# The first block of output weights split in four parts instead of one, in the last heads of a latent-attention layer

## The chip, the cores and the metric

The kernel runs as one program on one core of a Trainium2 chip. The metric is the device time of one execution in microseconds (us), as the median of several runs. Five engines work side by side, each through its own list of instructions in order, and they wait for one another on semaphores (counters that one engine raises and another waits for): TensorE (PE in the profile), VectorE (DVE), ScalarE (ACT), GpSimd (POOL) and SyncE (SP, which here issues DMAs).

## What is computed

The reference is a trunk of two layers over 512 tokens of width 1024, all in float32. The first layer is a multi-head latent attention with 16 heads, the second a sparse attention. The change lies at the end of the first layer's attention, where the output projection begins:

```python
def mla_mixer(h, pos, w_in, g_cq, w_uq, g_ckv, w_ukv, g_q, g_k, w_out):
    proj = h @ w_in
    c_q, c_kv, k_pe, z = jnp.split(proj, [...], axis=-1)
    q = (rms_norm(c_q, g_cq) @ w_uq).reshape(B, S, MLA_HEADS, MLA_QK)
    kv = (rms_norm(c_kv, g_ckv) @ w_ukv).reshape(B, S, MLA_HEADS, MLA_NOPE + MLA_V)
    ...
    o = causal_block_attention(q, k, v, MLA_QK ** -0.5)
    o = o.reshape(B, S, MLA_HEADS * MLA_V) * jax.nn.silu(z)
    return o @ w_out
```

`w_out` has 2048 rows (128 for each of the 16 heads) and 1024 columns.

## The kernel before

**Products in two pieces.** A float32 product is made of three matmuls (`mm3`, lines 97 to 99): each operand is split into a high piece (a rounded copy) and a low piece (the operand less its high piece), and high times high, high times low and low times high are summed. For weights the high piece `w_hi` is a copy on ACT and the low piece `w_lo` a subtraction on POOL. Weights come from memory in blocks of 512 rows by 512 columns, which lie in SBUF as 128 partitions by 4 times 512 elements (`KP` = 4); there are two buffers of each kind, `w_raw`, `w_hi`, `w_lo`, used in turn.

**Slots.** The attention runs in slots, one for each head and block of 128 queries: slot s is head s // 4 and query block s % 4, with 64 slots in all (`SLOTS0` = 64, `NT` = 4). Each engine has a function `step(s)` that writes out its share of slot s, and the list of its instructions is that of step after step; nothing else sets the order. The share of a late slot is:

- SP: two DMA transposes for the slot three further on, of queries (L1074) and keys (L1076), into `qkT`; the scores of that slot wait for them.
- PE: `scores(s)` (five matmuls into a bank, L97 to L99, L1255, L1256), in each fourth slot `values` of the head before (L1286), then `turn_probs(s - 1)` (transposes of the probabilities, L1269, and of the gate, L1276), which waits for the exponential of slot s - 1.
- DVE: `maximum(s)` (L2328: scores and mask, with the row minimum), `key_low` (L2309, L2311: the low pieces of a key tile, after ACT's high piece), `query_low`, `probs_out` or `gate` in every fourth slot, `turn_sum(s - 1)` (L2341).
- ACT: `key_high` (L1664), `probs_out(s - 1)` (L1685), `z_out` (L1696), `exponential(s)` (L1678).
- POOL: `scale_z` in the first two slots of a head (L2026), and factors for keys and queries in earlier slots.

**The first output products.** In the last eight slots the projections of queries and keys are over, and the output projection begins in the free banks. Its first block of weights, `mid[0]`, landed long before. ACT makes its high piece in slot 56 (`mid_high(0)`, L1741) and POOL its low piece in slot 57 (`mid_low(0)`, L2018), each as one instruction on 128 x 2048 elements. From slot 58 on ACT and DVE split one finished head's output in each slot into `o_hi` (L1751) and `o_lo` (L2354), and PE takes the first products of the first two token tiles in slot 60, behind the scores of slot 60 and ahead of `turn_probs(59)` (`first_products`, called by the table `first_at`). They wait for the whole low piece of the weights and for the first `o_lo`:

```python
if k == 0 and t == 0:
    pe.wait_ge(m_lo, 1)
    pe.wait_ge(q_scaled, H // 2 * NT)
...
if t == 0:
    pe.wait_ge(o_lo_made, k + 1)
```

In DVE's slot, `o_low` stands behind everything else of that slot, and so ahead of `maximum` of the next one; in ACT's slot, `o_high` stands behind the exponential.

Of the kernel before, what the change touches and what calls it, by code (L numbers as in the profile page):

```python
# [15 lines left out]
F32 = mybir.dt.float32  # L16
# [4 lines left out]
ACT = mybir.ActivationFunctionType  # L21
ALU = mybir.AluOpType
# [4 lines left out]
NT = SEQ // P  # L27
# [7 lines left out]
H = 16  # L35
# [30 lines left out]
KP = 4  # L66
# [35 lines left out]
def trunk(nc, x, positions, inv_freq, norm_g, mla_w_in, mla_g_cq, mla_w_uq, mla_g_ckv, mla_w_ukv,  # L102
          mla_g_q, mla_g_k, mla_w_out, nsa_w_in, nsa_g_q, nsa_g_k, nsa_pe_k, nsa_w1_k, nsa_w2_k,
          nsa_pe_v, nsa_w1_v, nsa_w2_v, nsa_w_out, out):
    with ExitStack() as whole:
# [30 lines left out]
        w_raw = [keep(f"w_raw{s}", [P, KP, CW]) for s in range(2)]  # L136
        w_hi = [keep(f"w_hi{s}", [P, KP, CW], F32R) for s in range(2)]
        w_lo = [keep(f"w_lo{s}", [P, KP, CW], F32R) for s in range(2)]
# [35 lines left out]
        with ExitStack() as layer:  # L174
            z_sb = at_slab("z_sb", 0, [P, NT, ZZ])
            with ExitStack() as ctx:
# [82 lines left out]
                q_done, q_squares, q_factors, q_scaled, q_rotated = (sem(n) for n in (  # L259
                    "q_done", "q_squares", "q_factors", "q_scaled", "q_rotated"))  # L260
                kv_done, k_squares, kv_out, k_factors, k_rotated = (sem(n) for n in (
                    "kv_done", "k_squares", "kv_out", "k_factors", "k_rotated"))
# [6 lines left out]
                SLOTS0, KV0, AHEAD = H * NT, -8, 3  # L269
# [1243 lines left out]
                def _(act):  # L1513
# [185 lines left out]
                    def step(s):  # L1699
                        if k_split(s) is not None:  # L1700
                            key_high(k_split(s))
                        if q_split(s) is not None:
                            query_high(q_split(s))
                        if q_tile(s - 1):
                            q_stats(q_tile(s - 1))
                        if k_tile(s):
                            kv_stats(k_tile(s))
                        if (q_weights(s) or 0) > 1:
                            split_q(q_weights(s))
                        if (k_weights(s) or 0) > 1:  # L1710
                            split_kv(k_weights(s))
                        if 1 <= s <= SLOTS0 and s % NT != 3:
                            probs_out(s - 1)
                        if s % NT in (1, 2) and NT < s < SLOTS0:
                            z_out(s - 1)
                        if 0 <= s < SLOTS0:
                            exponential(s)
                        if s == KV0 + 1:
                            z_leave(NB - 2)
                        if s == KV0 + 4:  # L1720
                            z_leave(NB - 1)
                        if s == KV0 + 5:
                            nc.scalar.activation(exp_junk[:, 0:1], minus_half[:, 0:1], ACT.Exp)
                        if s == SLOTS0 - 8:
                            mid_high(0)
                        if SLOTS0 - 6 <= s < SLOTS0 - 2:
                            o_high(s - SLOTS0 + 6)
                        if s == SLOTS0:
                            mid_high(1)
                        if s == SLOTS0 + 1:  # L1730
                            z_out(SLOTS0)

                    def mid_high(g):
                        act.wait_ge(m_landed[g % 2], 16 * (g // 2 + 1))
                        if g < 2:
                            act.wait_ge(kv_done, NT * (H - 1 + g))
                            act.wait_ge(q_done, NT * (H // 2 - 1 + g))
                        else:
                            act.wait_ge(m_done, NT * (g - 1))
                        width = mid[g][3]  # L1740
                        nc.scalar.activation(w_hi[g % 2][:, :, 0:width], w_raw[g % 2][:, :, 0:width],  # L1741
                                             ACT.Copy).then_inc(m_hi, 1)
# [169 lines left out]
                def _(pool):  # L1912
# [87 lines left out]
                    def rotate(m):  # L2000
# [11 lines left out]
                        nc.gpsimd.tensor_tensor(q[:, :, HALF0:ROPE], rot[:, 1], rot[:, 2], ALU.add).then_inc(q_rotated, 1)  # L2012
                        pool.wait_ge(q_rotated, m + 1)

                    def mid_low(g):
                        pool.wait_ge(m_hi, g + 1)
                        width = mid[g][3]
                        nc.gpsimd.tensor_tensor(w_lo[g % 2][:, :, 0:width], w_raw[g % 2][:, :, 0:width],  # L2018
                                                w_hi[g % 2][:, :, 0:width].bitcast(F32), ALU.subtract).then_inc(m_lo, 1)
# [8 lines left out]
                    def step(s):  # L2028
                        if s >= NT and s % NT < 2:
                            scale_z(s // NT - 1, s % NT)  # L2030
                        if s == KV0 + 4:
                            pool.wait_ge(z_used, NB)
                            o.link(nc.gpsimd.memset(no_low(2), 0.0))
                        if k_tile(s) is not None and s % 2:
                            k_factors_of(k_tile(s - 1))
                        if (q_tile(s - 1) or 0) >= NT - 1:
                            rotate(q_tile(s - 1))
                        if q_tile(s) is not None:
                            q_factor(q_tile(s))
                        if s == SLOTS0 - 7:  # L2040
                            mid_low(0)

                    slots(step)

# [555 lines left out]
```

## Time and profile before

| | |
|---|---|
| median of 3 runs | 854.2 us (853.71 to 854.38) |
| the profiled execution | 855.4 us |
| its span, first to last instruction | 853.6 us |
| mean granted TensorE clock | 0.994 of full speed |
| PE busy | 827.9 us, 97% of the span |
| DVE, ACT, POOL busy | 65%, 58%, 57% |

The profiled execution took 1.2 us more than the median of the runs, and 1.8 us of its time lie outside the span. A row of a timeline gives the start of an instruction in us from the span's start, its duration, engine, line, operation, output and inputs, and in brackets how long the engine had been idle before it and what ended that. A row with x4 merges four instructions that follow one another. An engine starts its next instruction a little before the one ahead has ended, so two rows of one engine may overlap by some 0.1 us.

### The profile page before, as it was taken

What the parts mean: (1) busy time and instruction counts of PE and PEld (TensorE: products, weight loads), DVE (VectorE), ACT (ScalarE), POOL (GpSimd) and SP (SyncE); (2) the same over time, 40 slices, a digit from 0 to 9 for tenths busy, and PEclk for the clock granted to TensorE, in tenths of its full rate; (3) what the DMA queues carried; (4) which work ended last, traced back from release to release, by engine and by line L of the source; (5) the groups of instructions that cost most, each with busy time, mean ns of one, the idle gap of its engine ahead of it and who ended that gap; (6) DMA issues with size and microseconds to landing.
All of it is one profiled execution on the core that took longest, in us unless ns stands there. A gap on an engine that the chain in (4) does not pass through costs nothing.

```text
span 853.6 us, 16381 instructions
## 1 busy us (share of the span) xinstructions
PE 827.9 (97%) x5785; PEld 686.6 (80%) x5785; DVE 552.8 (65%) x1544; ACT 493.1 (58%) x1183; POOL 484.2 (57%) x628
## 2 busy tenths in 40 slices
PE   6999998999999997999999999999999999999998
PEld 6999998888888885788888887778887677777786
DVE  4899988887887788461111113476789688888521
ACT  5446658887887886531334223444344889988620
POOL 2000315878887876344446343565674799999641
PEclk9999999899999999999999999999999999999999
DMA  6423232646456545242247222123312100100011
GB/s 220 134 88 96 80 115 82 132 118 117 94 126 118 124 83 130 69 141 78 74 119 156 94 65 82 51 99 105 98 51 99 50 2 3 51 2 3 2 50 49
DMA packets 100763, 73.60 MB, mean 86 GB/s; under 512 B 70197, under 2 KB 83786, under 8 KB 100682
## 3 DMA queue, kind: packets, MB, share of 16 engines
q1 hardware_dynamic: 100640, 72.55, 31.6%
q8 instruction: 46, 0.75, 0.4%
q14 instruction: 35, 0.29, 0.1%
q10 hardware_dynamic: 42, 0.01, 0.0%
HBM read 55.63 MB, written 2.10 MB: 68 GB/s over the span
## 4 chain that ended last, share of the span: by engine, by line
PE 79%; DVE 9%; ACT 5%; issue 3%; DMA 2%; SPq 1%; POOL 1%; ACTq 0%; DVEq 0%; POOLq 0%
PE bank L97 18%; PE bank L99 18%; PE bank L98 18%; PE bank L1286 3%; DVE w_lo L2198 2%; PE bank L510 2%; PE bank L492 2%; PE bank L519 2%; PE bank L511 2%; PE bank L1269 1%; DMA qkT<-k 1%; PE bank L599 1%; ACT prob L1678 1%; PE bank L600 1%; PE bank L598 1%
## 5 line engine op out<-in xcount | busy, mean ns | idle before, releaser
L2018 POOL TENSOR_TENSOR w_lo<-w_raw,w_hi 128x2048 fp32r<-128x2048 f32 (+1 forms) x26 | 118.4, 4554 | 124.2 <-ACT w_hi L1741 124.1
L97 PE MATMUL bank<-w_hi,h_hi 128*128 128x512 f32 (+3 forms) x472 | 171.4, 363 | 2.0 <-DVE h_lo L2118 1.0
L99 PE MATMUL bank<-w_hi,h_lo 128*128 128x512 f32 (+3 forms) x472 | 166.8, 353 | 0.0
L98 PE MATMUL bank<-w_lo,h_hi 128*128 128x512 f32 (+3 forms) x472 | 166.8, 353 | 0.0
L1741 ACT ACTIVATE w_hi<-w_raw 128x2048 fp32r<-128x2048 f32 (+1 forms) x26 | 49.2, 1892 | 94.0 <-PE bank L99 94.0
L97 PEld LDWEIGHTS bank<-w_hi,h_hi 128*128 128x128 f32 x472 | 88.8, 188 | 15.3 <-issue 3.7
L99 PEld LDWEIGHTS bank<-w_hi,h_lo 128*128 128x128 f32 x472 | 88.7, 188 | 11.5
L98 PEld LDWEIGHTS bank<-w_lo,h_hi 128*128 128x128 f32 x472 | 88.9, 188 | 10.1
L797 POOL TENSOR_TENSOR p<-kvr,p 128x512 f16<-128x512 f32 (+1 forms) x96 | 88.5, 942 | 10.3 <-ACT p L713 9.9
L97 PE MATMUL bank<-w_hi,c_hi 128*128 128x256 f32 (+1 forms) x224 | 78.6, 351 | 0.3 <-DVE w_lo L2277 0.2
L97 PE MATMUL bank<-w_hi,o_hi 128*128 128x512 f32 x192 | 77.7, 405 | 0.4 <-DVE o_lo L2354 0.4
L98 PE MATMUL bank<-w_lo,o_hi 128*128 128x512 f32 x192 | 76.2, 397 | 0.0
L99 PE MATMUL bank<-w_hi,o_lo 128*128 128x512 f32 x192 | 76.2, 397 | 0.0
L99 PE MATMUL bank<-w_hi,c_lo 128*128 128x256 f32 (+1 forms) x224 | 69.2, 309 | 0.0
L98 PE MATMUL bank<-w_lo,c_hi 128*128 128x256 f32 (+1 forms) x224 | 69.2, 309 | 0.0
L710 ACT ACTIVATE kvr<-bank,g_cols 128x512 f32<-128x512 f32 (+1 forms) x96 | 60.4, 630 | 7.6 <-PE bank L526 7.6
L847 DVE CUSTOM_DVE_ANT_0 scored<-bank,band 128x128 f32<-128x128 f32 (+3 forms) x128 | 56.1, 484 | 10.2 <-PE bank L492 10.2
L713 ACT ACTIVATE p<-bank,g_cols 128x512 f16<-128x512 f32 (+1 forms) x96 | 60.6, 631 | 0.0
L2328 DVE CUSTOM_DVE_ANT_0 below<-bank,band,g_cols 128x128 f32<-128x128 f32 (+1 forms) x64 | 34.8, 544 | 25.1 <-PE bank L1256 24.5
L97 PEld LDWEIGHTS bank<-w_hi,c_hi 128*128 128x128 f32 x224 | 43.1, 192 | 3.6 <-DVE w_lo L2277 0.5
L97 PEld LDWEIGHTS bank<-w_hi,o_hi 128*128 128x128 f32 x192 | 36.4, 189 | 8.8 <-issue 0.6
L98 PEld LDWEIGHTS bank<-w_lo,c_hi 128*128 128x128 f32 x224 | 43.1, 192 | 0.4
(362 smaller groups left out, 2336.7 us busy)
## 6 DMA issues: line engine op xcount, KB each, us to landing
w_raw<-in_nsa_w_in SPq DMA_DIRECT2D x10, 1024.0 KB, 5.0
w_raw<-in_mla_w_in SPq DMA_DIRECT2D x8, 1024.0 KB, 5.1
w_raw<-in_mla_w_out SPq DMA_DIRECT2D x8, 1024.0 KB, 5.1
w_raw<-in_nsa_w_in SPq DMA_DIRECT2D x8, 984.0 KB, 5.0
w_raw<-in_nsa_w_out SPq DMA_DIRECT2D x4, 1024.0 KB, 5.1
w_raw<-in_mla_w_uq SPq DMA_DIRECT2D x7, 576.0 KB, 4.5
w_raw<-in_mla_w_ukv SPq DMA_DIRECT2D x15, 256.0 KB, 2.9
w_raw<-in_mla_w_in SPq DMA_DIRECT2D x4, 704.0 KB, 5.7
```

What stands on the lines that cost most here:

```text
L97: nc.tensor.matmul(out, a[0], b[0], start=start, stop=False)
L98: nc.tensor.matmul(out, a[0], b[1], start=False, stop=False)
L99: return nc.tensor.matmul(out, a[1], b[0], start=False, stop=stop)
L492: nc.tensor.matmul(first_bank(k)[:, 0:nb * keys].rearrange("p (b c) -> p b c", b=nb), qT_hi[a][0:DK, tok], kT_hi[0:DK, b0:b0 + nb, n // HP ...
L710: nc.scalar.activation(p32(k, u), src, ACT.Exp, scale=score_scale[:, 0:1])
L713: nc.scalar.activation(piece_of(p1, n, u), src, ACT.Exp, scale=score_scale[:, 0:1]).then_inc(exp_done, 1)
L797: nc.gpsimd.tensor_tensor(piece_of(p2, n, u), p32(k, u), piece_of(p1, n, u), ALU.subtract).then_inc(sub_done, 1)
L847: last = nc.vector.tensor_tensor_reduce(scored[k % 2][:, w * keys:(w + 1) * keys], first_bank(k)[:, w * keys:(w + 1) * keys], band[:, SEQ ...
L1286: last = nc.tensor.matmul(o_bank[:, j * P:SEQ], kv_sb[:, h % 4 * NT + j, NOPE:WKV], probT[h % 2][:, j * ROW + j * P:j * ROW + SEQ], start= ...
L1741: nc.scalar.activation(w_hi[g % 2][:, :, 0:width], w_raw[g % 2][:, :, 0:width], ACT.Copy).then_inc(m_hi, 1)
L2018: nc.gpsimd.tensor_tensor(w_lo[g % 2][:, :, 0:width], w_raw[g % 2][:, :, 0:width], w_hi[g % 2][:, :, 0:width].bitcast(F32), ALU.subtract). ...
L2328: nc.vector.tensor_tensor_reduce(below[i % 2][:, 0:keys], score_bank[i % 2][:, 0:keys], band[:, SEQ - keys:SEQ], score_scale[:, 1:2], -LEA ...
```

## The change

The one high piece on ACT in slot 56 and the one low piece on POOL in slot 57 become four each, one k (128 x 512 elements) a slot, in slots 56 to 59 on both engines. ACT makes part k at the end of its slot 56 + k, ahead of `o_high` where that slot has one; POOL follows at the end of its own slot 56 + k. Only the first part on ACT waits for the block and for the buffers; only the fourth part on POOL raises `m_lo`, for which PE waits. Later blocks are as they were, but for POOL's count of `m_hi`.

```diff
@@ ScalarE, step(s)
-                        if s == SLOTS0 - 8:
-                            mid_high(0)
+                        if SLOTS0 - 8 <= s < SLOTS0 - 8 + KP:
+                            first_high(s - SLOTS0 + 8)
                         if SLOTS0 - 6 <= s < SLOTS0 - 2:
                             o_high(s - SLOTS0 + 6)
...
+                    def first_high(k):
+                        if k == 0:
+                            act.wait_ge(m_landed[0], 16)
+                            act.wait_ge(kv_done, NT * (H - 1))
+                            act.wait_ge(q_done, NT * (H // 2 - 1))
+                        width = mid[0][3]
+                        nc.scalar.activation(w_hi[0][:, k, 0:width], w_raw[0][:, k, 0:width], ACT.Copy).then_inc(m_hi, 1)
...
-                        if g < 2:
-                            act.wait_ge(kv_done, NT * (H - 1 + g))
-                            act.wait_ge(q_done, NT * (H // 2 - 1 + g))
+                        if g == 1:
+                            act.wait_ge(kv_done, NT * H)
+                            act.wait_ge(q_done, NT * H // 2)
...
@@ GpSimd
+                    def first_low(k):
+                        pool.wait_ge(m_hi, k + 1)
+                        width = mid[0][3]
+                        last = nc.gpsimd.tensor_tensor(w_lo[0][:, k, 0:width], w_raw[0][:, k, 0:width],
+                                                       w_hi[0][:, k, 0:width].bitcast(F32), ALU.subtract)
+                        if k == KP - 1:
+                            last.then_inc(m_lo, 1)
...
-                        pool.wait_ge(m_hi, g + 1)
+                        pool.wait_ge(m_hi, g + KP)
...
-                        if s == SLOTS0 - 7:
-                            mid_low(0)
+                        if SLOTS0 - 8 <= s < SLOTS0 - 8 + KP:
+                            first_low(s - SLOTS0 + 8)
```

The lists of PE, DVE and SP are the same as before. On ACT, slots 56 to 59 read as follows (`w_hi0`, `w_raw0`: the first buffers; `k16`: the key's high piece; `prob`: the exponential; `o_hi0`, `o_hi1`: the first two heads' outputs). Before:

```order
544 L1678 ACTIVATE prob_109,rowsum_64<-below0_107,negmax_63 128x128 [waits max_done]
545 L1741 ACTIVATE w_hi0<-w_raw0 128x2048 [waits q_done,kv_done,m_landed0]
546 L1664 ACTIVATE k16_1_72<-kv_sb_75,ms_k_67 128x128 [waits k_rotated,kv_out]
...
553 L1678 ACTIVATE prob_109,rowsum_64<-below0_107,negmax_63 128x384 [waits max_done]
554 L1751 ACTIVATE o_hi0_113<-z_sb_56 128x512 [waits o_free,q_done,kv_done]
555 L1678 ACTIVATE prob_109,rowsum_64<-below1_108,negmax_63 128x512 [waits max_done]
556 L1751 ACTIVATE o_hi1_114<-z_sb_56 128x512 [waits o_free]
557 L1685 ACTIVATE probT0_110<-bank2 128x4x128 [waits t_done]
```

and now:

```order
545 L1739 ACTIVATE w_hi0<-w_raw0 128x512 [waits q_done,kv_done,m_landed0]
...
549 L1678 ACTIVATE prob_109,rowsum_64<-below1_108,negmax_63 128x256 [waits max_done]
550 L1739 ACTIVATE w_hi0<-w_raw0 128x512
...
554 L1678 ACTIVATE prob_109,rowsum_64<-below0_107,negmax_63 128x384 [waits max_done]
555 L1739 ACTIVATE w_hi0<-w_raw0 128x512
556 L1759 ACTIVATE o_hi0_113<-z_sb_56 128x512 [waits o_free,q_done,kv_done]
557 L1678 ACTIVATE prob_109,rowsum_64<-below1_108,negmax_63 128x512 [waits max_done]
558 L1739 ACTIVATE w_hi0<-w_raw0 128x512
559 L1759 ACTIVATE o_hi1_114<-z_sb_56 128x512 [waits o_free]
```

The third part stands behind the exponential of slot 58, and the fourth behind that of slot 59; both stand ahead of an `o_hi`.

On POOL, the same slots (`z_sb`, `rinv`: `scale_z`). Before:

```order
368 L1995 TENSOR_TENSOR k16_1_72<-kpe_sb_59,ms_k_67 128x2x128 [waits x_landed1,x_landed0,k_factors]
369 L2026 TENSOR_TENSOR z_sb_56<-z_sb_56,rinv_65 128x2x128 [waits sum_turned] x2
370 L2018 TENSOR_TENSOR w_lo0<-w_raw0,w_hi0 128x2048 [waits m_hi]
371 L2026 TENSOR_TENSOR z_sb_56<-z_sb_56,rinv_65 128x2x128 [waits sum_turned] x4
372 L2018 TENSOR_TENSOR w_lo1<-w_raw1,w_hi1 128x2048 [waits m_hi]
```

and now:

```order
368 L2003 TENSOR_TENSOR k16_1_72<-kpe_sb_59,ms_k_67 128x2x128 [waits x_landed1,x_landed0,k_factors]
369 L2042 TENSOR_TENSOR z_sb_56<-z_sb_56,rinv_65 128x2x128 [waits sum_turned]
370 L2026 TENSOR_TENSOR w_lo0<-w_raw0,w_hi0 128x512 [waits m_hi]
371 L2042 TENSOR_TENSOR z_sb_56<-z_sb_56,rinv_65 128x2x128 [waits sum_turned]
372 L2026 TENSOR_TENSOR w_lo0<-w_raw0,w_hi0 128x512 [waits m_hi] x3
373 L2042 TENSOR_TENSOR z_sb_56<-z_sb_56,rinv_65 128x2x128 [waits sum_turned] x4
```

The second `scale_z` now stands behind the first part, and the last four behind the fourth part, which follows ACT's exponential of slot 59.

PE's list is unchanged; this is the place in it where the products stand, with the waits that they carry:

```order
2090 L1269 MATMUL bank2<-ident,prob_109 128x128 [waits zt_ready,pt_ready,exp_done]
2091 L1269 MATMUL bank2<-ident,prob_109 128x128 x2
2092 L97 MATMUL bank0<-qkT1_103 128x128 [waits max_done,x_landed0]
...
2097 L97 MATMUL bank4<-w_hi0,o_hi0_113 128x512 [waits o_lo_made,q_scaled,m_lo]
...
2103 L1269 MATMUL bank2<-ident,prob_109 128x128 [waits pt_ready,exp_done]
```

Nothing moved here: the transposes of slot 58's probabilities, the scores of slot 60, the six products, and behind them the transposes of slot 59's probabilities.

## Rows read from the trace of the kernel before

**Rows 1.** The profile's page: busy time by engine.

```profile
PE 827.9 (97%) x5785; PEld 686.6 (80%) x5785; DVE 552.8 (65%) x1544; ACT 493.1 (58%) x1183; POOL 484.2 (57%) x628
```

**Rows 2.** Waits, 325 to 370 us: waiter, releaser, total us, times, longest us.

```profile
PEld bank L1269 <- ACT prob L1678: 4.6, 3, 2.9
ACT prob L1678 <- DVE negmax L2328: 4.5, 3, 2.5
```

**Rows 3.** Timeline of POOL: the block's low piece; later, a piece of quarter size.

```profile
332.31 4.52 POOL L2018 TENSOR_TENSOR w_lo<-w_raw,w_hi 128x2048 fp32r<-128x2048 f32 x1 [0.50 <-ACT w_hi L1741]
...
684.08 1.26 POOL L788 TENSOR_TENSOR w_lo<-w_raw,w_hi 128x512 fp32r<-128x512 f32 x1
685.30 0.39 POOL L802 TENSOR_TENSOR c_s<-c_s,c_min 128x128 f32<-128x128 f32 x1
```

**Rows 4.** Timeline of DVE, slots 57 to 59.

```profile
332.56 4.42 DVE L2309 SCALAR_TENSOR_TENSOR k<-kv_sb,ms_k,k 128x128 f16<-128x128 f32 x1 [1.05 <-ACT k L1664]
336.90 0.27 DVE L2311 SCALAR_TENSOR_TENSOR k<-kpe_sb,ms_k,k 128x64 f16<-128x64 f32 x1
...
337.17 0.59 DVE L2328 CUSTOM_DVE_ANT_0 below<-bank,band,g_cols 128x384 f32<-128x384 f32 x1
...
337.69 0.34 DVE L2309 SCALAR_TENSOR_TENSOR k<-kv_sb,ms_k,k 128x128 f16<-128x128 f32 x1
...
339.07 0.69 DVE L2354 TENSOR_TENSOR o_lo<-z_sb,o_hi 128x512 fp32r<-128x512 f32 x1 [0.76 <-ACT o_hi L1751]
339.68 0.74 DVE L2328 CUSTOM_DVE_ANT_0 below<-bank,band,g_cols 128x512 f32<-128x512 f32 x1
```

**Rows 5.** Timeline of ACT, slots 56 to 59, and four copies in a row.

```profile
333.83 0.40 ACT L1664 ACTIVATE k<-kv_sb,ms_k 128x128 f16<-128x128 f32 x1
334.68 0.38 ACT L1685 ACTIVATE probT<-bank 128x256 f32<-128x256 f32 x1 [0.46 <-PE bank L1276]
334.96 0.38 ACT L1696 ACTIVATE zT<-bank 128x256 f32<-128x256 f32 x1
337.81 0.61 ACT L1678 ACTIVATE prob<-below,negmax 128x384 f32<-128x384 f32 x1 [2.47 <-DVE negmax L2328]
...
338.42 0.61 ACT L1751 ACTIVATE o_hi<-z_sb 128x512 fp32r<-128x512 f32 x1
340.46 0.72 ACT L1678 ACTIVATE prob<-below,negmax 128x512 f32<-128x512 f32 x1 [1.43 <-DVE negmax L2328]
...
341.19 0.61 ACT L1751 ACTIVATE o_hi<-z_sb 128x512 fp32r<-128x512 f32 x1
...
357.67 2.18 ACT L1751 ACTIVATE o_hi<-z_sb 128x512 fp32r<-128x512 f32 x4
```

**Rows 6.** Timeline of PE, slots 58 to 62.

```profile
333.35 0.33 PE L1256 MATMUL bank<-qkT 128*128 128x384 f16 x1
...
335.77 0.38 PE L1256 MATMUL bank<-qkT 128*128 128x512 f16 x1
338.57 0.55 PE L1269 MATMUL bank<-ident,prob 128*128 128x128 f32 x3 [2.42 <-ACT prob L1678]
...
339.90 0.77 PE L97 MATMUL bank<-w_hi,o_hi 128*128 128x512 f32 x1 [0.36 <-DVE o_lo L2354]
...
342.57 0.60 PE L1269 MATMUL bank<-ident,prob 128*128 128x128 f32 x4
...
347.12 0.53 PE L97 MATMUL bank<-w_hi,o_hi 128*128 128x512 f32 x1
...
348.64 0.38 PE L1269 MATMUL bank<-ident,prob 128*128 128x128 f32 x2
```

**Rows 7.** Stretches: busy us by engine, then granted TensorE clock, DMA share, GB/s.

```profile
339.40:340.20 0.80, 0.44 (x3) 0.33 (x2) 0.80 (x2) 0.00 (x0) 0.00 (x0) 0.50 0.73 149
...
344.20:345.00 0.80, 0.80 (x3) 0.37 (x2) 0.27 (x1) 0.50 (x1) 0.00 (x0) 1.00 0.19 37
```

**Rows 8.** Timeline of SP's queue: the key transpose for slot 60.

```profile
334.98 2.04 SPq L1076 DMA_TRANSPOSE qkT<-k  x1
```

## The prediction, made before the changed kernel ran

> **What bounds the kernel now.** I read the page first: PE is busy for 97% of the span [rows 1], so an edit matters only where PE stands idle or where it makes PE wait. Next come the waits around the slots that the change touches. Between 325 and 370 us PE's longest wait is for the exponential (ACT, L1678), and ACT's longest there is for DVE's maximum [rows 2]: 2.47 us on ACT and 2.42 us on PE end in one chain. The timelines then show what DVE did meanwhile. The low piece of a key, L2309, took 4.42 us [rows 4], where the next one of the same shape took 0.34. It started 0.25 us after POOL's low piece of the weight block (332.31, 4.52 us long [rows 3]), and DVE's next instruction started at 336.90, 0.07 us after POOL's end at 336.83. So a DVE instruction that reads two SBUF tensors stood still until POOL was done. Behind it stood the maximum of slot 58 (337.17), then the exponential (337.81), then PE's transposes (338.57) [rows 4, 5, 6]. The change makes four short holds out of the long one, and that should remove this wait. But the products of slot 60 (339.90) wait for the weights' low piece and for the first o_lo. Now the weights are ready at 336.83, three microseconds early, and o_lo ends last at 339.76 [rows 4, 6]. After the change the weights become ready only behind the exponential of slot 59. That is what the sum is about.
>
> **The path up to slot 58.** Part 0 on ACT starts where the large copy started; POOL's part 0 follows for 1.27 us, then scale_z. DVE's L2309 loses at most the rest of a part, and the maximum of slot 58 can start when its scores are ready, at 333.35 + 0.33 = 333.68 [rows 6]; with 0.59 us it ends near 334.3. Part 1 on ACT goes ahead of the key copy at 333.83, and 0.55 + 0.3 later, at about 334.7, the copy of turned probabilities starts as before, at 334.68, since it waits for PE [rows 5]. I cost this part at 0, with 0.1 at most. The second copy at 334.96 lasts 0.38, so the exponential of slot 58 starts at about 335.24 instead of 337.81: 2.57 us gained. Moving scale_z behind part 0 costs nothing, as PE's use of it is about 1.5 us away.
>
> **The path from there to the products.** In this order, each behind the one before:
> - The exponential with the read of its sum holds ACT for 338.42 - 337.81 = 0.61 us [rows 5], to 335.85.
> - Part 2 on ACT: four copies of 128 x 512 in a row took 2.18 us, 0.55 each [rows 5]; done at about 336.4. POOL starts 0.07 later, at 336.47.
> - Part 2 on POOL: 1.26 us for a subtraction of that shape [rows 3]; done at 337.73. The bounds are 4.52 / 4 = 1.13 and 1.3.
> - o_high(0) stands behind part 2 on ACT and ends near 336.98, when POOL is already in its part. o_low(0) reads two SBUF tensors (L2354), and as L2309 did it waits for POOL's end. L2309's 4.42 us, its own 0.34 counted from the end, reach to 336.98, 0.15 after POOL's end, so the work itself begins about 0.2 before POOL's recorded end. That puts o_low(0) at 337.6 to 338.3, and maximum(59) behind it at 338.25. Its scores had been ready since 336.15 [rows 6].
> - From the start of this maximum to that of its exponential: 340.46 - 339.68 = 0.78 us [rows 4, 5], giving 339.03. The exponential holds ACT for 341.19 - 340.46 = 0.73, to 339.76.
> - Part 3 on ACT 0.55 and hand-over 0.07: 340.4. Part 3 on POOL 1.26: 341.66. From a releaser's end to PE 339.90 - 339.76 = 0.14: the products start at 341.8.
>
> They started at 339.90. **The sum is +1.9 us for the start of the products.** The 2.57 us gained at slot 58 are spent, and 1.9 more, because the products had covered the maximum and the exponential of slot 59 before, and now wait for those, and then for one part on ACT and one on POOL.
>
> **What hangs on it.** Queued behind the products on PE are the transposes of slot 59's probabilities (342.57), which need only the exponential, and then scores and values. From 344.20 on PE is busy without a gap [rows 7], and so I find no place where the delay would be absorbed; the later blocks' pieces wait for PE. POOL's scale_z of the next head, behind part 3, ends by 342.6 and is needed some 5 us later. SP's list gates nothing new: the key transpose for slot 60 is issued at 334.98 for 2.04 us [rows 8], so scores(60) come at about 338.3, ahead of the products in any case. The extra 0.3 us of ACT work (4 x 0.55 against one copy) are in the terms above.
>
> **The clock.** The products of slot 60 ran at half the granted clock (0.50, the 1.2 GHz level), after the idle 2.42 us [rows 6, 7]. Six of them took 342.57 - 339.90 = 2.67 us, against 348.64 - 347.12 = 1.52 at full clock. In the new order PE is idle from about 336.5 to 338.3 and from 338.9 to 341.8, with one slot's scores between. So I expect the fall again, and its price of 1.15 us again, plus some 0.3 for the transposes and scores behind the products while the clock is still low. Bounds: -1.15 if the clock doesn't fall, +2.5 if values(14) too (about 2.3 us long at full clock) runs at half.
>
> The sum against the profiled execution is 855.4 + 1.9 + 0.3 = 857.6. The runs' median is 1.2 below that execution, and I carry the difference over: 854.2 + 2.2 = **856.4**.
>
> **A rule weighed.** The trace has quarter-size subtractions on POOL that last 1.26 us; the next instruction starts 1.22 us after the one shown [rows 3]. The Trainium skill, Perfetto Trace Analysis, in its passage on the GpSimd profiler boundary, says that a GpSimd span is unreliable and that start-to-start spacing is to be used; by that the two parts in the sum would cost 0.08 us less and the result would be 856.3. DVE's release within 0.07 us of POOL's recorded end [rows 3, 4] speaks for the spans here.
>
> **Rivals.**
> 1. *The clock stays up, or PE's wait is shorter than I think; not slower by what can be measured.* If the granted clock stays at 1.00 over the products, 1.15 us come back: 854.2 + 1.9 - 1.15 = 854.95. It decides at the point where the products start; for it speaks that PE has the three transposes and the scores of slot 60 spread over its idle time, against it that a shorter idle time (2.42 us) was enough before. Chance 0.25.
> 2. *o_low(0) gets in ahead of POOL's part 2.* The Trainium skill, SBUF — State Buffer, section "Who interferes with whom", has the instruction that starts first hold the shared port and the other wait in full; by this rule alone the order of starts decides, and the row on L2309 agrees. If o_low(0) started first, maximum(59) would start at 337.6, and the products at 341.15: +1.25, and with the clock term 855.75. ACT's order speaks against it, since part 2 leaves ACT 0.5 us before o_hi does. Chance 0.08.
> 3. *The long hold was worth more than its 2.57 us.* If the maximum and the exponential of slot 59 ran so early that the products start by 339.3, the shorter idle time would also keep the clock up: 339.3 - 339.9 - 1.15 = -1.75, so 852.4 or less. It decides at that start; against it stands the chain above, 6.5 us of work behind 335.24, so it needs a term that I have taken for work to be no work. Chance 0.07.
> 4. *The change doesn't do what it says:* DVE still stands still behind the parts in each slot, and the exponential of slot 58 comes at 336 or later. Each 0.5 us of it is 0.5 us more: 857 to 858. It counts with the forecast's side.
>
> **How the numbers follow.** The forecast, that the products wait for part 3 and the kernel ends 1.7 to 4 us later, has 0.60. A measurement of this kernel can tell about 0.2% from no change, which is 1.7 us: slower therefore starts at 855.9. Rival 2 lies within that bound, and so does rival 1. Chances: faster 0.07, same 0.33, slower 0.60. The range reaches down to rival 1, 854.9, and up to the longer stretch of low clock, 858.2.
>
> **What would show it.** In the profile of the changed kernel: no DVE L2309 above 1.3 us; the exponential of slot 58 near 335.2; an o_lo of about 1.3 us instead of 0.69; a wait of PE L97 of about 3 us in slot 60, ended by POOL's w_lo, where now 0.36 us end with DVE's o_lo; and products about 1.9 us later. It would be wrong if the products' wait ended with o_lo, or if the exponential of slot 59 came before about 338.5.

## The result, and the profile after

The changed kernel takes 857.73 us (median of 4 runs, 856.21 to 858.5) against 854.25 us before: a ratio of 1.0042, with a 95% interval of 1.003 to 1.0054. It is slower by 3.5 us, 2.6 to 4.6 by the interval. The prediction was 856.4, slower, in a range of 854.9 to 858.2. The profiled execution took 857.57 us, 2.2 us above that of before; its span is 855.8 us against 853.6.

The first waits between 325 and 372 us that end at PE or at the exponential, in the profile after (waiter, releaser, total us, times, longest):

```profile
PEld bank L97 <- POOL w_lo L2026: 4.0, 1, 4.0
PE bank L97 <- POOL w_lo L2026: 3.8, 1, 3.8
ACT prob L1678 <- DVE negmax L2344: 2.7, 2, 2.1
...
PEld bank L1269 <- ACT prob L1678: 2.1, 3, 1.0
...
PE bank L97 <- DMA qkT<-k: 1.2, 2, 1.0
PE bank L1269 <- ACT prob L1678: 1.2, 2, 0.9
```

In [rows 2] the longest of PE's waits was for the exponential, with a longest one of 2.4 us on the matmul side [rows 6]; now it is 3.8 us for the weights' low piece.

DVE after, slots 57 to 59 (lines from 1733 on have moved; L2325 and L2327 are the low key piece, L2344 the maximum, L2370 the output's low piece):

```profile
330.69 1.03 DVE L2325 SCALAR_TENSOR_TENSOR k<-kv_sb,ms_k,k 128x128 f16<-128x128 f32 x1
...
334.04 1.18 DVE L2325 SCALAR_TENSOR_TENSOR k<-kv_sb,ms_k,k 128x128 f16<-128x128 f32 x1 [0.44 <-ACT k L1664]
...
336.27 1.34 DVE L2370 TENSOR_TENSOR o_lo<-z_sb,o_hi 128x512 fp32r<-128x512 f32 x1 [0.78 <-ACT o_hi L1759]
337.53 0.74 DVE L2344 CUSTOM_DVE_ANT_0 below<-bank,band,g_cols 128x512 f32<-128x512 f32 x1
```

Of [rows 4], the key piece of slot 57 takes 1.03 us where it took 4.42, that of slot 58 takes 1.18 where it took 0.34, and the o_lo that took 0.69 takes 1.34: several short holds instead of one long one. The other end of the chain, on ACT and POOL:

```profile
334.49 0.61 ACT L1678 ACTIVATE prob<-below,negmax 128x384 f32<-128x384 f32 x1
...
338.31 0.72 ACT L1678 ACTIVATE prob<-below,negmax 128x512 f32<-128x512 f32 x1 [2.08 <-DVE negmax L2344]
...
339.03 0.61 ACT L1739 ACTIVATE w_hi<-w_raw 128x512 fp32r<-128x512 f32 x1
```

```profile
335.80 1.26 POOL L2026 TENSOR_TENSOR w_lo<-w_raw,w_hi 128x512 fp32r<-128x512 f32 x1 [0.72 <-ACT w_hi L1739]
339.72 1.26 POOL L2026 TENSOR_TENSOR w_lo<-w_raw,w_hi 128x512 fp32r<-128x512 f32 x1 [2.66 <-ACT w_hi L1739]
```

And PE, from the transposes of slot 56 to those of slot 60, in the profile after:

```profile
331.64 0.27 PE L1269 MATMUL bank<-ident,prob 128*128 128x128 f32 x1
...
341.04 0.79 PE L97 MATMUL bank<-w_hi,o_hi 128*128 128x512 f32 x1 [3.82 <-POOL w_lo L2026]
...
343.76 1.05 PE L1269 MATMUL bank<-ident,prob 128*128 128x128 f32 x4
...
345.68 2.73 PE L1286 MATMUL bank<-probT,kv_sb 128*128 128x512 f32 x8
348.24 0.27 PE L1269 MATMUL bank<-ident,prob 128*128 128x128 f32 x1
```

The same two ends, and values(14) between them, in the profile before:

```profile
332.37 0.27 PE L1269 MATMUL bank<-ident,prob 128*128 128x128 f32 x1
...
343.86 2.42 PE L1286 MATMUL bank<-probT,kv_sb 128*128 128x512 f32 x8
346.12 0.27 PE L1269 MATMUL bank<-ident,prob 128*128 128x128 f32 x1
```

Two executions arrive at slot 56 at different times, from differences far ahead of the change, so I count from one point: the start of slot 56's transposes on PE, 331.64 here and 332.37 in the profile before. From there the products start after 9.40 us (before: 339.90 - 332.37 = 7.53), and slot 60's transposes after 16.60 (before: 13.75). Of the 2.85 us, 1.87 lie ahead of the products and 0.98 between them and slot 60's transposes. The spans differ by 2.2 only, since the execution after reached slot 56 earlier by 0.73. Behind slot 60's transposes nothing differs: from their start to that of PE's last matmul all twelve traces of this case take 503.92 to 503.96 us. So what an edit does to the time of a profiled execution is over by then, and nothing behind it takes any of the delay back.

The granted clock (busy us by engine, then clock, DMA share, GB/s), first just behind the products in the profile before, then in four stretches of the profile after:

```profile
342.60:343.40 0.80, 0.80 (x9) 0.76 (x8) 0.27 (x3) 0.20 (x1) 0.45 (x1) 1.00 0.35 71
```

```profile
340.60:341.40 0.80, 0.36 (x1) 0.36 (x2) 0.80 (x1) 0.00 (x0) 0.80 (x2) 0.50 0.02 0
...
345.40:346.20 0.80, 0.80 (x4) 0.52 (x3) 0.00 (x0) 0.80 (x4) 0.00 (x0) 0.50 0.76 67
346.20:347.00 0.80, 0.80 (x3) 0.25 (x2) 0.62 (x2) 0.15 (x1) 0.00 (x0) 0.82 0.97 364
347.00:347.80 0.80, 0.80 (x4) 0.51 (x3) 0.55 (x4) 0.00 (x0) 0.00 (x0) 1.00 1.05 410
```

Before, the clock was back at 1.00 when the products were through. Now it stays at 0.50 over the four transposes behind them, the scores of slot 61 and the start of values(14), which takes 2.56 us to the next row instead of 2.26.

### The profile page after: what moved, and what is told of

It reads as the page before. It is cut to its first block, busy times and chain, and to the rows that moved or that the text cites. A ratio compares the mean times of both kernels' runs of the same rounds, so it can differ in the third digit from the quotient of the medians.

```text
span 855.8 us, 16387 instructions
## 1 busy us (share of the span) xinstructions
PE 827.2 (97%) x5785; PEld 686.0 (80%) x5785; DVE 552.3 (65%) x1544; ACT 493.2 (58%) x1186; POOL 482.5 (56%) x631
## 4 chain that ended last, share of the span: by engine, by line
PE 73%; ACT 4%; DMA 2%; DVE 2%; issue 1%; POOL 1%; SPq 0%; ACTq 0%; POOLq 0%; DVEq 0%
PE bank L97 16%; PE bank L99 16%; PE bank L98 16%; PE bank L1286 4%; PE bank L510 2%; PE bank L492 2%; PE bank L519 2%; PE bank L511 2%; PE bank L1269 2%; ACT prob L1678 1%; DMA qkT<-k 1%; PE bank L599 1%; PE bank L600 1%; PE bank L598 1%; PE bank L577 1%
## 5 line engine op out<-in xcount | busy, mean ns | idle before, releaser
L2034 POOL TENSOR_TENSOR w_lo<-w_raw,w_hi 128x2048 fp32r<-128x2048 f32 (+1 forms) x25 | 113.8, 4553 | 123.7 <-ACT w_hi L1749 123.6
L97 PE MATMUL bank<-w_hi,h_hi 128*128 128x512 f32 (+3 forms) x472 | 171.2, 363 | 2.1 <-DVE h_lo L2134 1.0
L1749 ACT ACTIVATE w_hi<-w_raw 128x2048 fp32r<-128x2048 f32 (+1 forms) x25 | 47.3, 1892 | 94.3 <-PE bank L99 94.3
L97 PEld LDWEIGHTS bank<-w_hi,h_hi 128*128 128x128 f32 x472 | 88.8, 188 | 15.4 <-issue 3.6
L97 PE MATMUL bank<-w_hi,o_hi 128*128 128x512 f32 x192 | 77.7, 405 | 3.8 <-POOL w_lo L2026 3.8
L97 PE MATMUL bank<-w_hi,c_hi 128*128 128x256 f32 (+1 forms) x224 | 78.2, 349 | 0.6 <-DVE w_lo L2293 0.5
L2344 DVE CUSTOM_DVE_ANT_0 below<-bank,band,g_cols 128x128 f32<-128x128 f32 (+1 forms) x64 | 34.7, 542 | 24.4 <-PE bank L1256 23.8
L97 PEld LDWEIGHTS bank<-w_hi,o_hi 128*128 128x128 f32 x192 | 36.4, 189 | 12.2 <-POOL w_lo L2026 4.0
L97 PEld LDWEIGHTS bank<-w_hi,c_hi 128*128 128x128 f32 x224 | 42.8, 191 | 3.7 <-DVE w_lo L2293 0.7
L99 PEld LDWEIGHTS bank<-w_hi,o_lo 128*128 128x128 f32 x192 | 36.4, 190 | 8.6
```

Of the source, the lines that this page charges most:

```text
L97: nc.tensor.matmul(out, a[0], b[0], start=start, stop=False)
L99: return nc.tensor.matmul(out, a[1], b[0], start=False, stop=stop)
L2344: nc.vector.tensor_tensor_reduce(below[i % 2][:, 0:keys], score_bank[i % 2][:, 0:keys], band[:, SEQ - keys:SEQ], score_scale[:, 1:2], -LEA ...
```

## The experiments

Each table entry counts from slot 56's transposes on PE, in the profiled execution; the ratio is that of the runs against the kernel before on the same chip. One execution of each kernel was profiled, and it need not be a typical one: that of e8 is the fastest of its eleven runs (852.87 us), that of e2 the slowest of its six (853.9).

| kernel | products start | slot 60's transposes | ratio (95%) |
|---|---|---|---|
| before | 7.53 | 13.75 | 1 |
| the change | 9.40 | 16.60 | 1.0042 (1.003 to 1.0054) |
| e1_change_again | 9.41 | 15.80 | 1.0031 (1.002 to 1.0042) |
| e4_output_first | 8.79 | 16.15 | 1.003 (1.0019 to 1.004) |
| e6_change_filled | 9.54 | 14.56 | 1.0019 (1.001 to 1.0028) |
| e8_last_two_together | 7.15 | 12.20 | 0.9994 (0.9985 to 1.0002) |
| e3_slot_earlier | 7.32 | 12.38 | 1.0007 (0.9996 to 1.0019) |
| e5_four_earlier | 5.79 | 10.85 | 1.0006 (0.9998 to 1.0014) |
| e7_before_filled | 7.53 | 12.56 | 0.9985 (0.9977 to 0.9994) |
| e2_low_only | 7.03 | 13.37 | 0.9972 (0.9961 to 0.9983) |
| e9_low_only_again | 6.92 | 13.19 | 0.9977 (0.9964 to 0.999) |
| e10_low_only_filled | 6.43 | 11.44 | 0.9968 (0.9955 to 0.998) |

In e5 and e3 parts stand ahead of slot 56, so the point from which the table counts comes late itself and their entries look too small. In e5 PE had waited 2.46 us for a copy of turned probabilities shortly ahead of it, and the values took 4.12 us instead of 2.42; in e3 the values began 1.21 us behind the scores of slot 57 instead of 0.85.

**The change once more.** No edit.

> The changed kernel unaltered, beside the others on one chip. My theory (products of slot 60 wait for part 3 of the weights, behind the exponential of slot 59): products start 9.4 us after the values step of slot 57's successor, that is about 11.7 us after the start of values(13), against 9.8 before; the time 3 to 3.5 us above the kernel before. If the 3.5 us of the first comparison were chance and only the 2.2 us between the two profiled executions real, this run shows about +2.2.

857.37 us against 854.55, +2.8 (1.7 to 3.6 by the interval): slower again, but between the 3 to 3.5 of the theory and the 2.2 of its rival, so this run doesn't decide how much. The products start after 9.41 us, to the hundredth as in the first profile; slot 60's transposes after 15.80 instead of 16.60. So the place of the products is fixed, and what follows varies by 0.8 us. Here the clock was already back for most of what follows:

```profile
340.40:343.20 2.80, 2.63 (x6) 2.04 (x7) 1.01 (x4) 0.00 (x0) 1.71 (x3) 0.50 0.41 82
343.30:344.70 1.40, 1.26 (x11) 0.93 (x9) 0.00 (x0) 0.65 (x2) 0.00 (x0) 0.92 0.48 100
```

The first stretch holds the products, at 0.50 again, and the second the transposes and scores behind them, at 0.92. Why the clock came back earlier here isn't shown.

**The last part a slot earlier, behind part 2.** Parts in slots 56, 57, 58 and 58.

```diff
-                        if SLOTS0 - 8 <= s < SLOTS0 - 8 + KP:
-                            first_high(s - SLOTS0 + 8)
+                        if SLOTS0 - 8 <= s < SLOTS0 - 5:
+                            first_high(s - SLOTS0 + 8)
+                        if s == SLOTS0 - 6:
+                            first_high(3)
```

and the same on POOL with first_low.

> The change with its last part one slot earlier, behind part 2: parts in slots 56, 57, 58 and 58 on both engines. No part stands ahead of slot 56, so nothing holds the low query piece. Theory (the loss is the wait for the part behind the exponential of slot 59): the weights are ready near 339.0 to 339.5 on the clock of the trace before, the products start about 2.2 us earlier than in the change, and the time is 3 us below the change, 0 to 1 us below the kernel before. Rival (four parts hold DVE and ACT more than one whole piece does): 1 us or more above the kernel before.

The products start after 7.15 us, 2.25 earlier than in the change, and the time is 854.25 against 854.65: the loss is gone. The wait is still there, but short:

```profile
338.47 0.51 PE L97 MATMUL bank<-w_hi,o_hi 128*128 128x512 f32 x1 [1.64 <-POOL w_lo L2028]
```

This is the test of the main step. The four parts, their holds of DVE and their extra work on ACT are all in this kernel; only the last part no longer stands behind the exponential of slot 59, and that is worth 3 us. The maximum of slot 59 even starts at the same place as in the change, 5.89 us after slot 56's transposes. The 3 us are not the earlier start alone (2.25): in this profile the clock stayed at 1.00 over the products, which took 1.50 us. The rival (parts as such cost more than the whole) falls.

**All four parts one slot earlier**, slots 55 to 58.

```diff
-                        if SLOTS0 - 8 <= s < SLOTS0 - 8 + KP:
-                            first_high(s - SLOTS0 + 8)
+                        if SLOTS0 - 9 <= s < SLOTS0 - 9 + KP:
+                            first_high(s - SLOTS0 + 9)
```

and the same on POOL with first_low.

> The change with all four parts one slot earlier, in slots 55 to 58 on both engines. My theory: part 3 now follows the exponential of slot 58 instead of 59, so the weights are ready near 337.7 and PE does not wait for them; the products start near 338.9 to 339: the 3.5 us of the change are gone and 1.0 us is gained against the kernel before, 2.1 if the clock stays up. Rival (the parts in the slots delay ACT and DVE wherever they stand): the time stays 1 us or more above the kernel before.

The wait for the weights is gone, and the 1 us of gain didn't come: 854.82 against 854.55, so the theory's number was missed on one side and the rival's on the other. PE now waited for a DMA; PE and SP's queue:

```profile
336.72 0.39 PE L97 MATMUL bank<-qkT 128*128 128x512 f16 x1 [2.05 <-DMA qkT<-k]
```

```profile
SPq L1073 <- DVE q L2335: 3.0, 1, 3.0
```

The key transpose for slot 59 came late because SP had waited 3.0 us for the low query piece, and on DVE that piece (L2334, L2335) took 0.85 and 1.36 us instead of 0.41 and 0.28: it stood beside POOL's scale_z and then beside POOL's second part (331.26, 1.46 us long):

```profile
330.73 0.85 DVE L2334 TENSOR_TENSOR q<-qn,q 128x256 f16<-128x256 f32 x1
331.50 1.36 DVE L2335 TENSOR_TENSOR q<-qn,q 128x128 f16<-128x128 f32 x1
```

The holds of DVE thus have a second customer, SP's transposes, as long as key and query tiles are still being made.

**Four slots earlier**, slots 52 to 55; the same edit with SLOTS0 - 12.

> The change with all four parts four slots earlier, in slots 52 to 55, so that the weights are ready before any output is split. Theory from the run with the parts one slot earlier (there PE waited 2.0 us for the key transpose of slot 59, since POOL's parts held DVE's low query piece, for which SP's transposes wait): here each part meets the low key and query pieces of a slot, so the transposes fall behind in slots 55 to 59; PE's wait for them is 3 us or more, and the time is that of the kernel before or up to 2 us above it. Rival (the one-slot-earlier run was only unlucky): 1 us or more faster than before.

855.0 against 854.65 (ratio 1.0006, 0.9998 to 1.0014). The time is as expected, the place isn't: between 310 and 345 us PE waited 1.9 us for transposes, not 3, and 2.5 us for a copy of turned probabilities on DVE (L2351), which stood behind a low key piece held for 1.29 us.

```profile
PE bank L1269 <- DVE probT L2351: 2.5, 1, 2.5
PE bank L97 <- DMA qkT<-k: 1.9, 3, 1.0
```

**The output ahead of the weights on ACT.** In slots 58 and 59 `o_high` and `first_high` are swapped:

```diff
-                        if SLOTS0 - 8 <= s < SLOTS0 - 8 + KP:
-                            first_high(s - SLOTS0 + 8)
                         if SLOTS0 - 6 <= s < SLOTS0 - 2:
                             o_high(s - SLOTS0 + 6)
+                        if SLOTS0 - 8 <= s < SLOTS0 - 8 + KP:
+                            first_high(s - SLOTS0 + 8)
```

> The change with one swap on ACT: in slots 58 and 59 the output's high piece goes ahead of the weights' part. My theory of the held o_lo (1.34 us instead of 0.69, because POOL's part starts first): DVE's o_lo starts first and lasts 0.69, the maximum of slot 59 and the products come about 1.2 us earlier than in the change, the last part being 0.55 us later on ACT but the maximum 1.2 earlier: 0.5 to 1.2 us faster than the change. Rival (the hold is hidden behind something else): the time is that of the change or 0.5 us above it, since part 3 stands 0.55 us later on ACT.

The mechanism is there: o_lo, then the maximum of slot 59:

```profile
335.93 0.69 DVE L2370 TENSOR_TENSOR o_lo<-z_sb,o_hi 128x512 fp32r<-128x512 f32 x1 [0.27 <-ACT o_hi L1759]
336.56 0.75 DVE L2344 CUSTOM_DVE_ANT_0 below<-bank,band,g_cols 128x512 f32<-128x512 f32 x1
```

From slot 56's transposes (331.81) the maximum starts after 4.75 us, against 337.53 - 331.64 = 5.89 in the change: 1.14 earlier. The products start 0.6 earlier (8.79 against 9.40), as 0.55 goes back to the later part. But the time is 857.24 against 857.37 of e1 on the same chip, where 0.5 to 1.2 us were expected: a gain of 0.6 can't be told from none in these runs. The hold of o_lo is shown in the trace, its price in the median is not.

**Work for PE in its idle time.** The clock term by itself, once on the change and once on the kernel before. The transposes read `x_sb` and write a free bank, and nothing reads them.

```diff
                         if k == 0 and t == 0:
+                            pe.wait_ge(q_scaled, H // 2 * NT)
+                            for n in range(32):
+                                nc.tensor.transpose(bank[7][:, n % 4 * P:(n % 4 + 1) * P], x_sb[:, n % 4, 0:P], ident[:, :])
                             pe.wait_ge(m_lo, 1)
-                            pe.wait_ge(q_scaled, H // 2 * NT)
```

> The change, with 32 transposes of 128 x 128 from x into a free bank on PE, behind the scores of slot 60 and ahead of the wait for the weights (some 3.5 us of work in an idle time of 3.8; their output is never read). Clock theory: the granted clock stays at 1.00 over the products, which take 1.5 us instead of 2.7, and the transposes and scores behind them run at full too: 1.5 to 2 us faster than the change, about 855.7. Rival (the lower clock costs nothing, since what follows waits for ACT anyway): within 0.5 us of the change. The products start 9.4 us after the transposes of slot 56 in both.

856.4 us, 1.0019 against 1.0031 of the change on its chip: about 1.0 us faster, less than the 1.5 to 2 expected, and the intervals overlap, so the medians alone don't settle it. In the profile the products ran at full clock and slot 60's transposes came after 14.56 us, 2.04 and 1.24 earlier than in the two profiles of the change, although the products themselves started 0.13 later; in this execution the added work ended after the weights were ready.

```profile
342.40:344.00 1.60, 1.60 (x10) 1.30 (x9) 0.67 (x4) 0.00 (x0) 1.37 (x2) 1.00 0.45 92
```

```diff
+                        if s == SLOTS0 - 6:
+                            pe.wait_ge(q_scaled, H // 2 * NT)
+                            for n in range(20):
+                                nc.tensor.transpose(bank[7][:, n % 4 * P:(n % 4 + 1) * P], x_sb[:, n % 4, 0:P], ident[:, :])
                         if s < SLOTS0:
                             pe.wait_ge(exp_done, s + 1)
```

> The kernel before, with 20 such transposes on PE (2.2 us) ahead of the wait for the exponential of slot 58, in the 2.4 us in which PE was idle. Clock theory: the fall to 0.50 over the products is gone, 1.0 to 1.2 us faster than before. Rival: the time of the kernel before.

853.45 against 854.65, a ratio of 0.9985 (0.9977 to 0.9994): 1.2 us faster with 20 useless transposes added. The products start at the same place, after 7.53 us, and slot 60's transposes 1.19 earlier. That is the price of the fall alone. The medians differ by as much (0.5 to 2.0 us by the interval), which speaks for the fall in typical executions of the kernel before, and not only in the profiled one.

```profile
336.12 2.35 PE L1264 MATMUL bank<-ident,x_sb 128*128 128x128 f32 x20
...
339.40 0.47 PE L97 MATMUL bank<-w_hi,o_hi 128*128 128x512 f32 x1 [0.32 <-DVE o_lo L2358]
```

```profile
339.40:341.00 1.60, 1.60 (x8) 1.19 (x9) 1.60 (x5) 1.05 (x3) 0.00 (x0) 1.00 0.44 91
```

**Only the low piece in four parts.** From the kernel before: ACT as it was, and POOL's parts one after another in slot 57.

```diff
+                    def first_low():
+                        pool.wait_ge(m_hi, 1)
+                        for k in range(KP):
+                            last = nc.gpsimd.tensor_tensor(w_lo[0][:, k, :], w_raw[0][:, k, :],
+                                                           w_hi[0][:, k, :].bitcast(F32), ALU.subtract)
+                        last.then_inc(m_lo, 1)
...
                         if s == SLOTS0 - 7:
-                            mid_low(0)
+                            first_low()
```

> Half of the change alone: ACT makes the high piece whole in slot 56 as before, POOL makes the low piece in four parts one after another, in slot 57, behind no exponential. My theory: the parts together take 5.0 us, so the weights are ready near 337.4 on the clock of the trace before, ahead of the first o_lo; DVE stands still one part at a time (1.0 to 1.3 us, possibly twice), the exponential of slot 58 comes 1.5 to 2.3 us earlier, and the products start when the scores of slot 60 are through, about 338.9: 1.0 us faster than before, 2.1 if the clock stays up. Rival (splitting the low piece costs as such, or DVE can't get in between parts that follow one another): DVE's low key piece still takes 4 us or more, and the time is that of the kernel before or slower.

> Again the kernel with only the low piece in four parts, since its 2.6 us below the kernel before rest on six runs, while the version with the last two parts together, whose products start as early, came out only 0.4 us below. If the gain is real: 1.5 to 3 us below the kernel before. If it was chance: 0.4 to 1.5 below.

851.97 us in the first batch (0.9972), 852.91 in the second (0.9977): 1.7 to 2.6 us faster than before, by medians. DVE gets in between parts that follow one another, one held instruction a part:

```profile
331.41 1.17 DVE L2316 SCALAR_TENSOR_TENSOR k<-kv_sb,ms_k,k 128x128 f16<-128x128 f32 x1 [1.07 <-ACT k L1664]
332.50 1.28 DVE L2318 SCALAR_TENSOR_TENSOR k<-kpe_sb,ms_k,k 128x64 f16<-128x64 f32 x1
```

```profile
331.16 5.05 POOL L2018 TENSOR_TENSOR w_lo<-w_raw,w_hi 128x512 fp32r<-128x512 f32 x4 [0.52 <-ACT w_hi L1741]
```

The exponential of slot 58 starts at 334.42, that is 3.20 us after slot 56's transposes (331.22), against 337.81 - 332.37 = 5.44 before. The products start only 0.5 us earlier, where 1.0 was expected. What PE waits for now is the key transpose of slot 60, behind a query transpose that took 2.10 us on SP's queue instead of 1.19:

```profile
337.99 0.23 PE L97 MATMUL bank<-qkT 128*128 128x128 f16 x1 [2.26 <-DMA qkT<-k]
```

**The same with work in that wait**: 16 transposes ahead of the scores of slot 60.

> The same kernel with 16 transposes of 128 x 128 into a free bank on PE (1.8 us), ahead of the scores of slot 60, in the 2.3 us in which PE waits for the key transpose of that slot. Clock theory: the granted clock no longer falls there in any run; 0.3 to 1.2 us faster than the same kernel without them, the most when many of its runs fell. Rival: no difference, or slower where the filler outlasts the idle time.

852.34 us against 854.66 (0.9968), against 852.91 without: 0.6 us, in the expected range, but inside the spread of the runs. In the profile slot 60's transposes come after 11.44 us instead of 13.19. By its ratio this is the fastest version, 2.3 us below the kernel before; its interval and that of e2, which has no useless work, overlap almost wholly, so no order of the two is shown.

**What stays open.** Where the gain of e2 and e9 comes from. In their profiles slot 60's transposes come 0.4 and 0.6 us earlier than before, and by the medians the kernels are 1.7 to 2.6 us faster. Both profiled executions are slow ones of their kind: 853.9 for a median of 851.97 in e2, 854.98 for 852.91 in e9, while e8's, at 852.87, is fast for its median of 854.25. So that e8 leads e2 in the table (12.20 against 13.37) and e2 leads e8 by 1.5 to 2 us in the medians is no contradiction, but no trace shows a typical execution of either. In e8's profile the clock didn't fall there and in e2's it did; over all runs the mean granted clock was 0.998 in five of e2's six and four of e9's eight, and in four of e8's eleven. That goes the right way, but it doesn't give the whole difference.

## Why the prediction was right, and what was mis-sized

**The direction and its reason: right.** The long hold of DVE went, the exponential of slot 58 came earlier, and the products had to wait for the part behind the exponential of slot 59. PE L97's wait changed from 0.36 us for o_lo to 3.82 us for w_lo (forecast: about 3). The extra 0.8 lies at its front and costs nothing: the forecast took over the slow key transpose of the trace before (2.04 us [rows 8]), this one took 1.26, and the scores of slot 60 came 0.8 us sooner than assumed.

**The path up to slot 58: right.** I had 2.57 us of gain for the exponential of slot 58. Counted from slot 56's transposes it started after 334.49 - 331.64 = 2.85 us instead of 5.44: 2.59. No time was lost to part 1 on ACT.

**The path to the products: right step by step, each within 0.08 us.** The forecast was +1.9 us; measured +1.87. Exponential and part 2 on ACT end and POOL starts after 335.80 - 334.49 = 1.31 us (forecast 1.23); POOL's part lasts 1.26; o_lo takes 1.34 and the maximum begins 1.26 after its start; from the maximum to its exponential 0.78, as taken from the rows. From that exponential to POOL's last part it took 339.72 - 338.31 = 1.41 instead of 1.35, and the last hand-over, from POOL's end to PE, 0.06 instead of 0.14. e8 shows the cause (the loss goes when the last part moves one slot), and e4 the hold of o_lo.

**What hangs on it: right, but SP mattered for variants.** That nothing absorbs the delay holds: behind slot 60's transposes the traces before and after agree to 0.03 us. The statement that scores(60) come ahead of the products was right too (336.76 against 341.04). e3 and e5 show what I hadn't weighed: had the parts stood earlier, SP's transposes (e3) or a copy on DVE behind a held key piece (e5) would have become the bound.

**The clock: the mis-sized term.** I had its fall again, at the same 1.15 us, and "some 0.3" for what comes behind the products. The products did take 2.72 us. What lies between them and slot 60's transposes took 0.93 us more than before: the four transposes 0.85 us to the next row instead of 0.43, scores and copy 1.07 instead of 0.86, and values(14) 2.56 instead of 2.26. So the term was 0.98 in this execution, 0.17 in e1's, where the clock was back within the transposes, over 2 us sooner. My upper bound of +2.5 held it, the value taken didn't. With 0.98 for 0.3 the sum would have been 857.1.

**The profiled sum: partly luck.** The forecast for the profiled execution was 857.6, and it took 857.57. Two misses cancel in it: the clock cost 0.7 us more than I took, and this execution reached slot 56 earlier by 0.73, which no term had and which isn't the change's doing. In the traces of the kernels with no edit ahead of slot 56 that point lies anywhere between 331.16 and 332.81.

**The rest, 857.1 to 857.73,** is not traced. I carried over the 1.2 us between the profiled execution and the median of before as if they were the same for both kernels, and gave no reason. For the changed kernel the profiled execution (857.57) lay at the median. Part of the 1.2 belongs to the few runs of the first comparison: in three later batches, of 12 to 35 runs, the median of the kernel before was 854.55 to 854.66, not 854.25, and against the first of these the change was 2.8 us slower. That the median runs of the kernel before had no fall of the clock is unlikely, since e7 took the fall away and its median gained about the full price, 1.2 us.

**The rivals.** 1, the clock stays up: it didn't in the two profiles of the change. e6 forced it and gave back about 1 us; what was left, 1.0019 (1.001 to 1.0028), is still slower, but about as little as the 1.7 us that I had set as the least that can be told. 2, o_lo first: it didn't happen, and e4 gave it by an edit; it brought the products forward by 0.6 us. That is near the 0.65 of the rival, but by another sum (the maximum 1.14 earlier, the last part 0.55 later), so it doesn't confirm the rival's number. 3, faster: not. 4, the exponential of slot 58 late: not.

## What to carry to other kernels

Splitting a long GpSimd instruction so that VectorE can get in between paid here (1.7 to 2.6 us in e2 and e9), but the pieces need no slots of their own: VectorE got in between pieces that stood back to back. Spreading them over the steps of a pipeline ties the last piece to everything that the engines do in order before it, and its consumer then loses the work that used to cover its neighbours' latency. Before moving such a piece, find who waits for the last one, and ask which exponential, copy or transfer now stands ahead of it; then ask it for each earlier place too, since a hold that is free in one slot stopped the transposes' input in another.

## What the runs showed of the hardware

- VectorE instructions with two SBUF inputs stood still for the rest of a running GpSimd subtraction (1.03 to 1.34 us instead of 0.34 and 0.69), and one that read a PSUM bank did not: the maximum of slot 58 took 0.59 us in the midst of e2's four parts, and 0.59 before with no part beside it. With four such GpSimd instructions in a row, each held VectorE instruction lost at most the rest of one of them: 1.17, 1.28, 0.78 and 1.29 us, not 5.05. The Trainium skill, SBUF — State Buffer, section "Who interferes with whom", says that a VectorE instruction with two SBUF inputs contends with a GpSimd instruction that reads SBUF, and that the order of issue decides which of them blocks. The traces agree, and they show as well that the blocked one gets its turn at the next border between instructions. GpSimd can then lose time in its turn: in e8 an o_lo of 0.83 us came in at the border of two parts, and the two took 2.94 us instead of 2 x 1.26.
- 2.35 us of useless transposes in an idle time of TensorE made a kernel 1.2 us faster, as the granted clock stayed at 1.00 over the next 1.5 us of products.
- Of the DMA transposes on SP's queue, which take 1.2 to 1.26 us, one around slots 56 to 61 takes 1.96 to 2.14 us in the traces of before, after, e2, e4 and e8 (2.31 in e10, and none of them in e3), and which one differs: the key transpose of slot 60 before [rows 8], a query transpose in the other four. In e4 the scores of slot 59 waited 1.18 us for a transpose, against 0.25 in the kernel before. I have no cause for it.
